# A transformer kernel's opening stage: weights loaded first, key slots parted into halves, and work moved between VectorE and ScalarE

## The chip, the cores and the metric

The kernel runs on one core of a Trainium2 chip. The metric is the device time of one execution in microseconds, as a median over runs. All arithmetic is fp32. Matrix products are made from split operands: each fp32 number is a rounded part (hi, in the fp32r format) and the rest (lo), and three products (hi x hi, lo x hi, hi x lo) stand for one.

## The reference, cut to what matters

The program is two transformer blocks over 256 tokens of width 2048, with 256 context tokens beside them in the first. The change touches the start of the first block:

```python
c_act = silu(c);  cc_act = silu(c_ctx)
mod = (c_act @ w_mod + b_mod)                 # 2048 -> 6 * 2048, for x
mod_c = (cc_act @ w_mod + b_mod)              # the same for the context
sh1, sc1, gt1, sh2, sc2, gt2 = split(mod, 6)
h  = rmsnorm(x,   g_norm1) * (1 + sc1)  + sh1
hc = rmsnorm(ctx, g_norm1) * (1 + csc1) + csh1
z  = h @ w_in                                 # keys, values, queries, gates of the mixers
```

rmsnorm divides by the root of the mean square over the 2048 features. So before the first key can be summed, the norm of x and ctx (the two streams, s = 0 and 1) and the first quarter of sh1 and sc1 must be there.

## The kernel before, in words

Weights come in slots of 1 MB (128 partitions x 2048 fp32). SyncE loads them into a ring of four raw buffers (RAW, `load`, L443 to L473). ScalarE rounds each half slot to hi (`front_split`, L537), VectorE subtracts to get lo (L1167), and TensorE uses both. There are two hi and two lo buffers of a slot each, so four halves can be ready or in use: the hi of half n waits until half n - 4 is used. A load waits until the second half of the slot that last held its raw buffer has been split (lo_ready). SyncE issues loads in one order, that of the first use of each slot, and waits in that order too.

The order of all halves is written out by hand in the list UNITS (L76 on). An entry is a kind, a number and a half, and its place in the list is called a unit here. Units 0 to 15 are the eight modulation slots of round 0; rounds 1, 2 and 3 have eight more each. A round gives one quarter of sh1 and sc1 for both streams. A modulation half is 4 matmuls of 128x512 on a 16-wide stationary operand (`mod_slot`, L2049, L2050), a key half 24 matmuls of 128x512 (`both`, L1965 to L1967). "key4" q is the part of four key columns that uses quarter q of the operand; "lr_key" 0 uses quarters 0 and 1. In the list of before each key4 slot stands whole: key4 0 at units 28 and 29, key4 1 and lr_key 0 at 46 to 49, key4 2 at 70 and 71, and then key 5 and key4 3.

All engines walk the same list. At each unit ScalarE and VectorE split the half four units further on (`ahead_of`), which on ScalarE waits until the present unit is used. Around that, at fixed places:

- Start: x and ctx are loaded in eight pieces of 0.5 MB ahead of all weights (L477). ScalarE squares them (L556), TensorE sums the squares over partitions with a matrix of ones (L2184), all ahead of the first modulation product. ScalarE takes the root at slot 1 (L515), VectorE the reciprocal at slot 3 (L1101).
- Norm product (L1319): two slots ahead of a round's end VectorE multiplies quarter r of both streams by the reciprocal root, 128x1024 each.
- End of a round: ScalarE copies the summed modulation rows out of PSUM (`mrows`, L572), TensorE turns them with eight small matmuls (`turn_rows`, L2057), VectorE adds the bias (`modulation`, L1179), makes the gain (`gains`, L1205) and applies the affine step, eight blocks of 128x256 (L1273, `operand_made`). ScalarE rounds the quarter of each stream to hi (L561, `operand_hi`), and VectorE makes the rest (L1280, `operand_rest`) one slot later, with two more lo halves between the two.

Of the kernel before, what the change touches and what calls it, by code (L numbers as in the profile page):

```python
# [23 lines left out]
ALU = mybir.AluOpType  # L24
ACT = mybir.ActivationFunctionType
AX = mybir.AxisListType.X

P = 128
# [47 lines left out]
UNITS = modulation_of(MODS[0] + MODS[1][:6]) + whole(("key4", 0)) + modulation_of(MODS[1][6:] + MODS[2][:6])  # L76
UNITS += whole(("key4", 1), ("lr_key", 0)) + modulation_of(MODS[2][6:] + MODS[3]) + whole(("key4", 2)) + [("key", 5, 0)]
# [25 lines left out]
LAST = [AT["mod", m[-1]] for m in MODS[:4]]  # L103
# [82 lines left out]
SHARED["made"] = [("x1", 8), ("y", 2), ("n2", 4), ("lat", 2)]  # L186
# [44 lines left out]
def build(nc, A, out):  # L231
    with ExitStack() as ctx:
        sems = {}

        def sem(name):
            if name not in sems:
                sems[name] = ctx.enter_context(nc.semaphore(name))
            return sems[name]
# [162 lines left out]
        def blk(t, j, n=1):  # L401
            return t[:, bass.ds(j * T, n * T)] if not isinstance(j, int) else t[:, j * T:(j + n) * T]
# [38 lines left out]
        def _(sp):  # L441
# [32 lines left out]

            for s in range(2):
                for q in range(4):
                    sp.dma_start(xs(xf, s, q), A["xt"][:, (s * KD + 4 * q) * T:(s * KD + 4 * q + 4) * T]).then_inc(sem(f"x_loaded{4 * s + q}"), 16)  # L477
            for t, (kind, k) in enumerate(FIRST_USE):
                load(t, t % RING, kind, k)
# [9 lines left out]
        def _(act):  # L489
# [63 lines left out]
            for s in range(2):  # L553
                for q in range(4):
                    act.wait_ge(sem(f"x_loaded{4 * s + q}"), 16)
                    act.activation(blk(sq[s], 4 * q, 4), xs(xf, s, q), ACT.Square).then_inc(sem("squares_ready"), 1)  # L556
            def operand_hi(r):

                for s in range(2):
                    act.wait_ge(sem("operand_made"), reached("made", "x1", 2 * r + s + 1))  # L560
                    act.activation(xs(xh, s, r), xs(xf, s, r), ACT.Copy).then_inc(sem("operand_hi"), 1)  # L561
# [3 lines left out]
            for u, (kind, k, half) in enumerate(UNITS):  # L565
                n = AT[kind, k]
                if half and n in LAST:
                    r = LAST.index(n)
# [4 lines left out]
                if (kind, k, half) == ("key4", 2, 1):  # L573
                    operand_hi(3)
# [7 lines left out]
                if n == 1:  # L582
                    root("n1", rsx[:, :], PS[4][:, :], D)
                for r in range(3):
                    if n == LAST[r] + 2:
                        operand_hi(r)

# [496 lines left out]
        def _(dve):  # L1084
# [179 lines left out]
            def operand_made(r):  # L1264

                modulation(r)
                for s in range(2):
                    gains(s, 16, s, "g1", 4 * r, 4)
                own.wait()
                for s in range(2):  # L1270
                    for b in range(4 * r, 4 * r + 4):
                        f = s * KD + b
                        ins = dve.tensor_scalar(blk(xf, f), blk(xf, f), amod[:, f:f + 1], mview[:, b, s:s + 1], ALU.mult, ALU.add)  # L1273
                    ins.then_inc(sem("operand_made"), 1)
# [20 lines left out]
            for u, (kind, k, half) in enumerate(UNITS):  # L1295
# [6 lines left out]
                if (kind, k, half) == ("key4", 2, 1):  # L1302
                    operand_made(3)
                    operand_rest(3)
                if UNITS[u] in HALF:
                    for m in ahead_of(u):
                        front_split(m)
                    if HALF[UNITS[u]] + 4 >= len(SPLITS) and not half:
                        split("mix_out", 0, (HALF[UNITS[u]] + 4 - len(SPLITS)) // 2, 0)
                if not half:  # L1310
                    continue
                if n == 3:
                    recip("n1", rsx[:, :])

                for r in range(4):
                    if n == LAST[r] - 2:
                        for s in range(2):
                            a = by_head(xs(xf, s, r))
                            own.done(dve.tensor_tensor(a, a, rsx[:, s * T:(s + 1) * T][:, None, :].to_broadcast([P, 4, T]), ALU.mult))  # L1319
                    if n == LAST[r] + 1 and r < 3:  # L1320
                        operand_made(r)
                    if n == LAST[r] + 2 and r < 3:
                        operand_rest(r)
# [224 lines left out]
            dve.wait_ge(sem("n2_gained"), 16)  # L1548
# [408 lines left out]
        def _(pe):  # L1957
# [222 lines left out]
            for s in range(2):  # L2180
                for b in range(KD):
                    if b % 4 == 0:
                        pe.wait_ge(sem("squares_ready"), reached("squares", "n1", 4 * s + b // 4 + 1))
                    ins = pe.matmul(PS[4][:, s * T:(s + 1) * T], ones[:, :], blk(sq[s], b), start=s + b == 0, stop=s == 1 and b == KD - 1,  # L2184
                                    skip_group_check=True)
            ins.then_inc(sem("norm_sum"), 1)
            pe.wait_ge(sem("c_ready"), 1)
            pe.wait_ge(sem("fold_ready"), 2)
            for t, (kind, k, half) in enumerate(UNITS):
# [43 lines left out]
                if AT[kind, k] - 1 in LAST and half == (kind != "key4"):  # L2233
                    turn_rows(LAST.index(AT[kind, k] - 1))
# [406 lines left out]
```

## Time and profile before

| | |
|---|---|
| Runs | 2837.6, 2826.0, 2834.99 us; median 2834.99 us |
| Profiled execution | 2836.49 us, span 2834.7 us, mean granted clock 0.979 |
| TensorE matmul busy | 2700.3 us (95%) |
| VectorE busy | 2027.8 us (72%) |
| ScalarE busy | 1421.4 us (50%) |
| DMA | 530.21 MB, mean 187 GB/s |

The stage that the change touches is the first 172 us. A busy share over the whole span says little of it; it is read by windows. "Idle before" a group is time in which its engine had nothing to do ahead of those instructions, with what ended it. The granted clock of TensorE is given as a share of its full 2.4 GHz; its other level is 0.5.

### The profile page before, as it was taken

How to read it: one execution, taken by the hardware profiler on the slowest of the kernel's cores; microseconds unless marked ns; L12 is line 12 of the kernel's file. 1: busy time of each engine (PE TensorE's matmuls, PEld its weight loads, DVE VectorE, ACT ScalarE, POOL GpSimd, SP SyncE). 2: the span in 40 equal slices, each digit the busy share in tenths (PEclk: the TensorE clock that was granted, in tenths of full speed). 3: DMA queues.
4: the chain of work that ended last, by engine and by line, in shares of the span. 5: the costliest groups of instructions: out<-in, count | busy, mean ns of one | idle time of the engine just before them, and what ended most of it. 6: DMA issues, size and time to landing. Idle time of an engine off the chain costs nothing.

```text
span 2834.7 us, 42305 instructions
## 1 busy us (share of the span) xinstructions
PE 2700.3 (95%) x15974; PEld 2343.9 (83%) x15974; DVE 2027.8 (72%) x3081; ACT 1421.4 (50%) x2000; POOL 0.2 (0%) x4
## 2 busy tenths in 40 slices
PE   7899999999979999999999999999999899999988
PEld 3468778998868888888888888889988898988877
DVE  6676786985878888887556777776654888456576
ACT  6433433444445555554444665554444654665563
POOL 0000000000000000000000000000000000000000
PEclk9999999999989999999999999999999999999989
DMA  8667565640735545455555455544555445432433
GB/s 345 226 250 268 228 258 220 220 186 31 268 137 189 191 179 191 181 191 175 189 189 189 170 186 191 179 172 182 183 188 183 146 160 186 165 136 109 178 139 129
DMA packets 104534, 530.21 MB, mean 187 GB/s; under 512 B 8240, under 2 KB 8784, under 8 KB 51296
## 3 DMA queue, kind: packets, MB, share of 16 engines
q1 hardware_dynamic: 101888, 515.93, 49.8%
q10 hardware_dynamic: 2528, 12.66, 1.2%
q8 instruction: 79, 1.29, 0.2%
q14 instruction: 39, 0.32, 0.0%
HBM read 526.46 MB, written 2.10 MB: 186 GB/s over the span
## 4 chain that ended last, share of the span: by engine, by line
PE 66%; DVE 7%; issue 3%; ACT 2%; ACTq 0%; DVEq 0%; DMA 0%
PE ps L1973 33%; PE ps L1974 16%; PE ps L1965 4%; PE ps L1967 4%; PE ps L1966 4%; DVE lo L1096 2%; ACT hi L503 1%; PE ps L2310 1%; DVE ws L1691 1%; PE ps L2481 1%; PE ps L2479 0%; PE ps L2315 0%; ACT L866 0%; DVE R L1739 0%; DVE O L1737 0%
## 5 line engine op out<-in xcount | busy, mean ns | idle before, releaser
L1096 DVE TENSOR_TENSOR lo<-raw,hi 128x1024 fp32r<-128x1024 f32 x700 | 843.3, 1222 | 480.5 <-ACT hi L503 477.7
L503 ACT ACTIVATE hi<-raw 128x1024 fp32r<-128x1024 f32 x700 | 732.3, 1056 | 615.6 <-PE ps L1974 547.1
L1973 PE MATMUL ps<-x,hi 128*128 128x512 f32 x1376 | 487.6, 400 | 0.0
L1974 PE MATMUL ps<-x,lo 128*128 128x256 f32 x1376 | 387.0, 281 | 0.0
L1973 PE MATMUL ps<-y,hi 128*128 128x512 f32 x1024 | 364.2, 400 | 3.6 <-DVE y L1943 3.6
L1973 PE MATMUL ps<-xp,hi 128*128 128x512 f32 x1024 | 358.6, 396 | 5.5 <-DVE lo L1096 3.7
L1973 PEld LDWEIGHTS ps<-x,hi 128*128 128x128 f32 x1376 | 259.3, 188 | 64.8
L537 ACT ACTIVATE hi<-raw 128x1024 fp32r<-128x1024 f32 x162 | 167.3, 1054 | 275.7 <-PE ps L1967 115.4
L1974 PE MATMUL ps<-y,lo 128*128 128x256 f32 x1024 | 288.9, 282 | 0.0
L1974 PE MATMUL ps<-xp,lo 128*128 128x256 f32 x1024 | 284.7, 278 | 0.0
L1167 DVE TENSOR_TENSOR lo<-raw,hi 128x1024 fp32r<-128x1024 f32 x162 | 192.5, 1220 | 104.8 <-ACT hi L537 104.7
L1974 PEld LDWEIGHTS ps<-x,lo 128*128 128x128 f32 x1376 | 260.6, 189 | 0.0
L1973 PE MATMUL ps<-hx,hi 128*128 128x512 f32 x688 | 243.1, 399 | 0.0
L1973 PEld LDWEIGHTS ps<-xp,hi 128*128 128x128 f32 x1024 | 192.0, 188 | 53.9 <-DVE lo L1096 6.9
L1973 PEld LDWEIGHTS ps<-y,hi 128*128 128x128 f32 x1024 | 194.0, 189 | 51.2 <-issue 4.1
L1974 PEld LDWEIGHTS ps<-y,lo 128*128 128x128 f32 x1024 | 195.3, 191 | 0.0
L1974 PE MATMUL ps<-hx,lo 128*128 128x256 f32 x688 | 193.2, 281 | 0.0
L1974 PEld LDWEIGHTS ps<-xp,lo 128*128 128x128 f32 x1024 | 192.6, 188 | 0.0
L1965 PE MATMUL ps<-xh,hi 128*128 128x256 f32 (+1 forms) x528 | 168.1, 318 | 5.6 <-ACT V L606 3.2
L1966 PE MATMUL ps<-xl,hi 128*128 128x256 f32 (+1 forms) x528 | 165.9, 314 | 0.0
L1967 PE MATMUL ps<-xh,lo 128*128 128x256 f32 (+1 forms) x528 | 165.8, 314 | 0.0
L1200 DVE SCALAR_TENSOR_TENSOR wsum<-raw,csil,wsum 128x512 f32<-128x512 f32 x210 | 157.6, 750 | 6.3
(385 smaller groups left out, 5015.3 us busy)
## 6 DMA issues: line engine op xcount, KB each, us to landing
raw<-in_weights SPq DMA_DIRECT2D x483, 1024.0 KB, 4.8
wlast<-in_weights ACTq DMA_DIRECT2D x8, 1024.0 KB, 4.8
xf<-in_xt SPq DMA_DIRECT2D x8, 512.0 KB, 9.5
raw<-in_weights SPq DMA_DIRECT2D x4, 768.0 KB, 4.3
R<-in_xt ACTq DMA_DIRECT2D x1, 2048.0 KB, 7.3
out<-R SPq DMA_DIRECT2D x1, 2048.0 KB, 6.3
maskn<-in_maskn ACTq DMA_DIRECT2D x1, 512.0 KB, 3.4
ptr<-in_pt ACTq DMA_DIRECT2D x2, 256.0 KB, 3.8
```

The lines of the kernel that those rows point to most:

```text
L503: act.activation(HI[p % PAIR][:, c], RAW[p % RING][:, c], ACT.Copy).then_inc(hi_ready, 1)
L537: act.activation(half_of(HI, n), RAW[t % RING][:, h * SLOT // 2:(h + 1) * SLOT // 2], ACT.Copy).then_inc(hi_ready, 1)
L1096: dve.tensor_tensor(LO[p % PAIR][:, c], RAW[p % RING][:, c], HI[p % PAIR][:, c].bitcast(F32), ALU.subtract).then_inc(lo_ready, 1)
L1167: dve.tensor_tensor(half_of(LO, n), RAW[t % RING][:, h * SLOT // 2:(h + 1) * SLOT // 2], half_of(HI, n).bitcast(F32), ALU.subtract).then_i ...
L1200: ins = dve.scalar_tensor_tensor(total[:, :], piece, scale, total[:, :], ALU.mult, ALU.add)
L1691: st.done(dve.tensor_tensor(dst[:, 16:UPW], src[:, 16:UPW], src[:, 16 - lag:UPW - lag], ALU.add))
L1965: pe.matmul(o, wh, ah, start=start, stop=False, **kw)
L1966: pe.matmul(o, wh, al, start=False, stop=False, **kw)
L1967: return pe.matmul(o, wl, ah, start=False, stop=stop, **kw)
L1973: pe.matmul(o, h, pair[:, :, k, :], start=start, stop=False, **kw)
L1974: return pe.matmul(o[:, 0, :], l, pair[:, 0, k, :], start=False, stop=stop, **kw)
L2310: pe.matmul(PS[4 + d][:, j * T:(j + 1) * T], W[:, t * T + j * P:t * T + (j + 1) * P], V[:, vc:vc + DV], start=(j, t) in ((0, 0), (1, 1 if ...
```

## The change

Five edits:

1. SyncE issues the first four weight slots ahead of the eight pieces of x. The squares and their sums, on ScalarE and TensorE, are parted into four groups of two pieces: squares after the splits made at units 1, 3, 5, 7, sums after units 3, 5, 7, 9. The root moves to unit 9 and the reciprocal to unit 11.
2. In UNITS the two halves of key4 0, key4 1, lr_key 0 and key4 2 are set apart, with modulation halves between. The second half follows the last modulation half of a round, at units 33, 45, 53 and 71 (45 is inside round 2). key4 0's first half is unit 26, key4 1's 40, lr_key 0's 48, key4 2's 64.
3. The rows of a round are turned inside the unit that follows the round, after two of its eight products where that is a key half, after the unit where it is a modulation half.
4. The affine step of stream 0 goes to ScalarE (four activations with scale and bias, 128x256 each, at the head of `operand_hi`); VectorE keeps stream 1. ScalarE waits for a new semaphore, gains_made. `operand_rest` follows `operand_made` directly, both at the unit behind the round.
5. The norm product of rounds 1 to 3 moves up to units 26, 40 and 48 (round 0: unit 13).

The core of the diff:

```diff
+UNITS = modulation_of(MODS[0] + MODS[1][:5]) + [("key4", 0, 0)] + modulation_of(MODS[1][5:]) + [("key4", 0, 1)]
+UNITS += modulation_of(MODS[2][:3]) + [("key4", 1, 0)] + modulation_of(MODS[2][3:5]) + [("key4", 1, 1)]
+UNITS += modulation_of(MODS[2][5:6]) + [("lr_key", 0, 0)] + modulation_of(MODS[2][6:]) + [("lr_key", 0, 1)]
+UNITS += modulation_of(MODS[3][:5]) + [("key4", 2, 0)] + modulation_of(MODS[3][5:]) + [("key4", 2, 1), ("key", 5, 0)]
...
+ENDS = [UNIT["mod", m[-1], 1] for m in MODS[:4]]
+NORMED_AT = [UNIT["mod", MODS[0][6], 1], UNIT["key4", 0, 0], UNIT["key4", 1, 0], UNIT["lr_key", 0, 0]]
+SQUARES_AT = [3, 5, 7, 9]
...
+            for t in range(RING):
+                load(t, t, *FIRST_USE[t])
             for s in range(2):
                 for q in range(4):
                     sp.dma_start(xs(xf, s, q), ...)
-            for t, (kind, k) in enumerate(FIRST_USE):
-                load(t, t % RING, kind, k)
+            for t in range(RING, len(FIRST_USE)):
+                load(t, t % RING, *FIRST_USE[t])
...
             def operand_hi(r):
+                act.wait_ge(sem("gains_made"), r + 1)
+                for b in range(4 * r, 4 * r + 4):
+                    ins = act.activation(blk(xf, b), blk(xf, b), ACT.Identity, scale=amod[:, b:b + 1], bias=mods[:, 2 * b:2 * b + 1])
+                ins.then_inc(sem("n2_gained"), 1)
...
+                if u - 1 in ENDS:
+                    operand_hi(ENDS.index(u - 1))
+                if u in ENDS:
+                    r = ENDS.index(u)
                     act.wait_ge(halves_used, HALF[kind, k, half] + 1)
                     if r:
                         act.wait_ge(sem("mod_turned"), r)
                     act.activation(mrows[:, :], PS[6 + r % 2][0:16, :], ACT.Copy).then_inc(sem("mod_rows"), 1)
                 if UNITS[u] in HALF:
                     for m in ahead_of(u):
                         front_split(m)
+                if u + 2 in SQUARES_AT:
+                    x_squares(SQUARES_AT.index(u + 2))
+                if u == SQUARES_AT[-1]:
+                    root("n1", rsx[:, :], PS[4][:, :], D)
...
             def operand_made(r):
                 modulation(r)
-                for s in range(2):
-                    gains(s, 16, s, "g1", 4 * r, 4)
+                gains(1, 16, 1, "g1", 4 * r, 4)
+                dve.scalar_tensor_tensor(amod[:, 4 * r:4 * r + 4], mview[:, 16 + 4 * r:20 + 4 * r, 0], 1.0, v("g1", 4 * r, 4),
+                                         ALU.add, ALU.mult).then_inc(sem("gains_made"), 1)
...
                 pe.wait_ge(lo_ready, m + 1)
                 for n in range(count // 2):
+                    if n == 2 and u - 1 in ENDS:
+                        turn_rows(ENDS.index(u - 1))
...
+                if t - 1 in ENDS and kind == "mod":
+                    turn_rows(ENDS.index(t - 1))
+                if t in SQUARES_AT:
+                    x_sums(SQUARES_AT.index(t))
```

`x_squares(n)` squares pieces 2n and 2n + 1 of x; `x_sums(n)` is eight of the 32 matmuls with ones.

## Rows read from the trace of the kernel before

**Rows 1.** The page: the span.
```profile
span 2834.7 us, 42305 instructions
```

**Rows 2.** Windows by round: stretch and length, busy time by engine, PEclk, DMA share, GB/s.
```profile
22.87:46.28 23.41, 18.21 (x66) 5.73 (x64) 21.51 (x18) 17.37 (x18) 0.00 (x0) 0.93 0.91 363
46.28:82.16 35.88, 29.91 (x121) 16.01 (x120) 27.29 (x34) 20.67 (x22) 0.00 (x0) 0.90 0.71 263
82.16:129.86 47.70, 40.12 (x169) 24.89 (x168) 30.76 (x37) 22.66 (x24) 0.00 (x0) 0.96 0.61 220
129.86:155.93 26.07, 18.50 (x72) 6.78 (x72) 25.72 (x33) 17.77 (x19) 0.00 (x0) 0.93 0.79 293
155.93:171.80 15.87, 13.47 (x56) 10.99 (x57) 10.77 (x19) 5.51 (x6) 0.00 (x0) 0.89 0.48 173
171.80:300.00 128.20, 128.20 (x660) 108.07 (x658) 93.62 (x116) 45.10 (x54) 0.00 (x0) 1.00 0.69 267
```

**Rows 3.** Groups of TensorE, 0 to 200 us: busy, mean ns | idle before.
```profile
L2049 PE MATMUL ps<-hi,cwin 128*16 128x512 f32 x128 | 55.0, 430 | 26.3 <-DVE lo L1167 25.9
...
L2057 PE MATMUL ps<-fold,mrows 16*128 16x8 f32 x32 | 4.2, 254 | 0.0
```

**Rows 4.** Timeline of ScalarE, 18 to 38 us: start, length, instruction, idle before.
```profile
18.99 2.00 ACT L537 ACTIVATE hi<-raw 128x1024 fp32r<-128x1024 f32 x2 [1.43 <-DMA raw<-in_weights]
...
28.47 1.28 ACT L515 ACT_TABLE_LOAD   x1
29.76 0.69 ACT L515 ACTIVATE rsx<-ps,vec 128x512 f32<-128x512 f32 x1
...
36.99 2.00 ACT L537 ACTIVATE hi<-raw 128x1024 fp32r<-128x1024 f32 x2 [0.46 <-DMA raw<-in_weights]
```

**Rows 5.** Groups of VectorE by form, 0 to 200 us.
```profile
L1167 DVE TENSOR_TENSOR lo<-raw,hi 128x1024 fp32r<-128x1024 f32 x80 | 93.4, 1219 | 50.0 <-ACT hi L537 49.8
...
L1273 DVE TENSOR_SCALAR xf<-xf,amod,mods 128x256 f32<-128x256 f32 x32 | 10.7, 406 | 0.1
...
L1101 DVE RECIPROCAL rsx<-rsx 128x512 f32<-128x512 f32 x1 | 3.3, 3343 | 0.0
...
L1205 DVE SCALAR_TENSOR_TENSOR amod<-mods,vec 128x4 f32<-128x4 f32 x8 | 0.9, 159 | 0.1
```

**Rows 6.** Groups of ScalarE by form, 0 to 200 us; L787 from the whole span.
```profile
L572 ACT ACTIVATE mrows<-ps 16x512 f32<-16x512 f32 x4 | 2.3, 570 | 0.0
...
L787 ACT ACTIVATE x<-tn,mods 128x256 fp32r<-128x256 f32 x16 | 6.7, 496 | 5.4 <-DVE tn L1552 5.4
```

**Rows 7.** Windows of TensorE: norm sums, four key halves, four modulation halves.
```profile
11.30:22.80 11.50, 11.50 (x55) 1.00 1.02 420
104.48:126.16 21.68, 21.68 (x97) 1.00 0.51 187
126.24:129.86 3.62, 3.62 (x16) 1.00 0.27 36
```

**Rows 8.** Loads of L473, issue to landing: 117 to 129 us, then 22 to 37 us.
```profile
DMA to landing us min/median/max: 4.7/4.7/4.7
...
DMA to landing us min/median/max: 5.6/6.4/7.0
```

**Rows 9.** Timeline of VectorE, 36 to 200 us: where the halves of each round stand.
```profile
43.91 2.35 DVE L1319 TENSOR_TENSOR xf<-xf,rsx 128x1024 f32<-128x1024 f32 x2
...
60.66 5.76 DVE L1167 TENSOR_TENSOR lo<-raw,hi 128x1024 fp32r<-128x1024 f32 x5
...
97.54 6.89 DVE L1167 TENSOR_TENSOR lo<-raw,hi 128x1024 fp32r<-128x1024 f32 x6
...
145.24 6.89 DVE L1167 TENSOR_TENSOR lo<-raw,hi 128x1024 fp32r<-128x1024 f32 x6
```

**Rows 10.** TensorE at unit 70: first matmul in the timeline, window over the half.
```profile
158.33 0.77 PE L1965 MATMUL ps<-xh,hi 128*128 128x512 f32 x1 [2.40 <-DVE lo L1167]
...
158.33:165.42 7.09, 7.09 (x25) 0.79 0.74 258
```

More of the change, by code:

```diff
@@ L102 @@
 UNIT = {e: n for n, e in enumerate(UNITS)}
-LAST = [AT["mod", m[-1]] for m in MODS[:4]]
+ENDS = [UNIT["mod", m[-1], 1] for m in MODS[:4]]
+NORMED_AT = [UNIT["mod", MODS[0][6], 1], UNIT["key4", 0, 0], UNIT["key4", 1, 0], UNIT["lr_key", 0, 0]]
+SQUARES_AT = [3, 5, 7, 9]
 NEXT_GATE = {n - 1: k for n, (kind, k) in enumerate(FRONT) if kind == "gate"}
@@ L185 @@
 SHARED["whole"] = [("up", KF), ("pool_in", 64), ("mla_in", 14), ("ple1", 16)]
-SHARED["made"] = [("x1", 8), ("y", 2), ("n2", 4), ("lat", 2)]
+SHARED["made"] = [("x1", 4), ("y", 2), ("n2", 4), ("lat", 2)]
 for _k in ("hi", "x"):
@@ L552, in _, with x_squares @@
             act.activation(csil[:, :], v("c2", 0, 2 * KD), ACT.Silu).then_inc(sem("c_act"), 1)
-            for s in range(2):
-                for q in range(4):
-                    act.wait_ge(sem(f"x_loaded{4 * s + q}"), 16)
+            def x_squares(n):
+                for m in (2 * n, 2 * n + 1):
+                    s, q = m // 4, m % 4
+                    act.wait_ge(sem(f"x_loaded{m}"), 16)
                     act.activation(blk(sq[s], 4 * q, 4), xs(xf, s, q), ACT.Square).then_inc(sem("squares_ready"), 1)
             def operand_hi(r):
+                act.wait_ge(sem("gains_made"), r + 1)
+                for b in range(4 * r, 4 * r + 4):
+                    ins = act.activation(blk(xf, b), blk(xf, b), ACT.Identity, scale=amod[:, b:b + 1], bias=mods[:, 2 * b:2 * b + 1])
+                ins.then_inc(sem("n2_gained"), 1)
                 for s in range(2):
-                    act.wait_ge(sem("operand_made"), reached("made", "x1", 2 * r + s + 1))
+                    if s:
+                        act.wait_ge(sem("operand_made"), reached("made", "x1", r + 1))
+                    else:
+                        act.wait_ge(sem("n2_gained"), r + 1)
                     act.activation(xs(xh, s, r), xs(xf, s, r), ACT.Copy).then_inc(sem("operand_hi"), 1)
@@ L566, in _ @@
                 n = AT[kind, k]
-                if half and n in LAST:
-                    r = LAST.index(n)
+                if u - 1 in ENDS:
+                    operand_hi(ENDS.index(u - 1))
+                if u in ENDS:
+                    r = ENDS.index(u)
                     act.wait_ge(halves_used, HALF[kind, k, half] + 1)
@@ L572, in _ @@
                     act.activation(mrows[:, :], PS[6 + r % 2][0:16, :], ACT.Copy).then_inc(sem("mod_rows"), 1)
-                if (kind, k, half) == ("key4", 2, 1):
-                    operand_hi(3)
                 if UNITS[u] in HALF:
@@ L579, in _ @@
                         split("mix_out", 0, (HALF[UNITS[u]] + 4 - len(SPLITS)) // 2, 0)
+                if u + 2 in SQUARES_AT:
+                    x_squares(SQUARES_AT.index(u + 2))
+                if u == SQUARES_AT[-1]:
+                    root("n1", rsx[:, :], PS[4][:, :], D)
                 if not half:
                     continue
[L582 to L586, printed above, removed]
                 if (kind, k) == ("key4", 3):
@@ L1266, in operand_made @@
                 modulation(r)
-                for s in range(2):
-                    gains(s, 16, s, "g1", 4 * r, 4)
+                gains(1, 16, 1, "g1", 4 * r, 4)
+                dve.scalar_tensor_tensor(amod[:, 4 * r:4 * r + 4], mview[:, 16 + 4 * r:20 + 4 * r, 0], 1.0, v("g1", 4 * r, 4),
+                                         ALU.add, ALU.mult).then_inc(sem("gains_made"), 1)
                 own.wait()
[L1270 to L1274, printed above, removed]
+                for b in range(4 * r, 4 * r + 4):
+                    f = KD + b
+                    ins = dve.tensor_scalar(blk(xf, f), blk(xf, f), amod[:, f:f + 1], mview[:, b, 1:2], ALU.mult, ALU.add)
+                ins.then_inc(sem("operand_made"), 1)
             def operand_rest(r):
@@ L1301, in _ @@
                     level_arg(m)
-                if (kind, k, half) == ("key4", 2, 1):
-                    operand_made(3)
-                    operand_rest(3)
+                if u - 1 in ENDS:
+                    operand_made(ENDS.index(u - 1))
+                    operand_rest(ENDS.index(u - 1))
                 if UNITS[u] in HALF:
@@ L1309, in _ @@
                         split("mix_out", 0, (HALF[UNITS[u]] + 4 - len(SPLITS)) // 2, 0)
+                if u == SQUARES_AT[-1] + 2:
+                    recip("n1", rsx[:, :])
+                if u in NORMED_AT:
+                    r = NORMED_AT.index(u)
+                    for s in range(2):
+                        a = by_head(xs(xf, s, r))
+                        ins = dve.tensor_tensor(a, a, rsx[:, s * T:(s + 1) * T][:, None, :].to_broadcast([P, 4, T]), ALU.mult)
+                        own.done(ins)
                 if not half:
                     continue
[L1312 to L1323, printed above, removed]
                 for g, end in enumerate(GROUP_ENDS):
@@ L1547, in _ @@
             recip("n2", rs[:, :])
-            dve.wait_ge(sem("n2_gained"), 16)
+            dve.wait_ge(sem("n2_gained"), 20)
             for q in range(5):
@@ L2179, in _, with x_sums @@
             pe.wait_ge(sem("ones_ready"), 1)
[L2180 to L2186, printed above, removed]
+            def x_sums(n):
+                for m in (2 * n, 2 * n + 1):
+                    pe.wait_ge(sem("squares_ready"), reached("squares", "n1", m + 1))
+                    s, q = m // 4, m % 4
+                    for b in range(4 * q, 4 * q + 4):
+                        ins = pe.matmul(PS[4][:, s * T:(s + 1) * T], ones[:, :], blk(sq[s], b), start=s + b == 0, stop=s == 1 and b == KD - 1,
+                                        skip_group_check=True)
+                if n == 3:
+                    ins.then_inc(sem("norm_sum"), 1)
             pe.wait_ge(sem("c_ready"), 1)
@@ L2231, in _ @@
                     half_slot(t, lambda n, h, l: one_stream(k % 2, n, h, l))
-                if AT[kind, k] - 1 in LAST and half == (kind != "key4"):
-                    turn_rows(LAST.index(AT[kind, k] - 1))
+                if t - 1 in ENDS and kind == "mod":
+                    turn_rows(ENDS.index(t - 1))
+                if t in SQUARES_AT:
+                    x_sums(SQUARES_AT.index(t))
                 if not half:
```

2 lines of the change are left out of this document (removed).

## The prediction

> **What bounds the kernel now.** I read the page first [rows 1], for the span against which the sum is made: 2834.7 us, in an execution that took 2836.49 us, 1.5 us above the median shown (2834.99). Then the windows [rows 2], cut where one modulation round ends and the next begins, since the diff touches nothing behind unit 71. From 171.8 us on TensorE has no free time (128.20 us busy of 128.20): what is won or lost ahead of that point passes whole into the span. Ahead of it TensorE is not the bound. Between 22.87 and 46.28 us VectorE is busy 21.51 of 23.41 us, between 129.86 and 155.93 us it is 25.72 of 26.07 us. In the two middle rounds it idles only while a key slot is on TensorE. The groups of TensorE [rows 3] say the same from the other side: 26.3 us idle ahead of modulation products, 25.9 us of that until a lo half was ready. Those 26 us are all that the change can win: 0.9% of the span. The start has a third bound, the DMA engines: the first weight slot lands at 18.99 us, the eighth at 36.99 us [rows 4], so (36.99 - 18.99) / 7 = 2.57 us for each MB.
>
> **Prices.** A lo half is 1.22 us alone [rows 5], 6.89 / 6 = 1.15 us in a row; the norm product is 2.35 us for both streams [rows 9]; one affine block is 10.7 / 32 = 0.33 us, a small operation on gains 0.16 us, the reciprocal 3.34 us [rows 5]. On ScalarE a hi half is 2.00 / 2 = 1.0 us [rows 4], the modulation rows 0.57 us, and a scaled, biased block of the same shape, from a later stage, 6.7 / 16 = 0.42 us [rows 6]. On TensorE a half of a key slot is 21.68 / 4 = 5.4 us, a modulation half 3.62 / 4 = 0.91 us, and the norm sums, at full clock, 11.50 / 55 = 0.21 us a record, so 3.4 us for the 16 records of one of the four new groups [rows 7]. Turning the rows is 4.2 / 4 = 1.05 us [rows 3]. A load that finds the queue empty lands 4.7 us after its issue [rows 8]; behind others 2.5 us more each.
>
> **Weights ahead of x, and norm sums between units 3 and 9.** The bytes ahead of slot 4 are the same 8 MB in either order. With 2.57 us for each MB and the first MB at about 7 us (an estimate from the same rate, counted back), slots 0 to 3 land by 17 us, x by 27 us, slot 4 at about 29 us and slot 7 at about 37 us, as now. That is why the early start wins nothing by itself. But ScalarE rounds both halves of slot 4 (to 31.4 us) ahead of x's third pair of squares (to 33.4), slot 5's halves (to 35.4) ahead of the fourth (to 37.4). TensorE sums the third pair to 35.9 us, does units 8 and 9 (to 37.8) and sums the fourth to 41.2. The root (0.7 us) stands on ScalarE ahead of the halves of slot 7, so these are split at 45.2 us and the reciprocal ends at 48.6 us. Before, VectorE had as many halves and the reciprocal behind it at 43.91 us [rows 9]. **Loss: 4.7 us** of VectorE time. The table load goes ahead of root's wait (1.28 us [rows 4]), so I put it at nothing. What the page would add: the Trainium skill, ScalarE: Activation LUTs, section What ACT_TABLE_LOAD costs, counts a drain of some 1.4 us with each switch; the rows show none, root starting as the load ends, and with it this term would be 6.1 us.
>
> **Half of the affine step on ScalarE.** VectorE loses four blocks a round (4 x 0.33 = 1.3 us). But operand_rest now follows operand_made at once, with no lo halves between them, and its first half waits for ScalarE: four blocks (1.7 us), a hi (1.0 us) and two hand-overs (0.2 us) behind gains_made, against 1.3 us of VectorE's own blocks. VectorE idles about 1.6 us, so the term is +0.3 us a round. Behind this wait stand all further splits of VectorE, and ScalarE, waiting for gains_made, holds back its own. Bounds: -1.3 us a round (the wait hidden) and +1.6 us (nothing saved).
> First anchor: the rests of round 0 end at 48.6 + 4 halves 4.6 + norm product 2.3 + four small operations 0.6 + 1.3 + wait 1.6 + two rests 2.3 = 61.3 us with 20 halves split; before, 60.66 us with 24 [rows 9]. Lag 0.6 + 4 x 1.15 = 5.2 us.
>
> **Key quarters in two halves.** The intention is plain: while TensorE works 5.4 us on a key half, VectorE catches up. With four buffers for halves it can be three ahead (3.4 us) and then idles, once per half instead of once per slot. So each half hides 3.4 us, and a slot parted hides twice that. Against it stand three things. The norm product for the next quarter comes behind the split that waits for this very key half (unit 30 behind 26), so its 2.3 us lie beside short modulation halves, not under the key. Second, raw slot 13 of the order, the first key quarter, is now held from unit 26 to 33; SyncE waits in order, so the load for units 34 and 35 is issued only when unit 33 is split. Third, that lands ahead of a wait: ScalarE's list has the rounding of units 34 and 35 ahead of the copy of the modulation rows of unit 32, and TensorE now asks for those rows inside unit 33, two products in. Counting from unit 29 used: hi 1.0 + lo 1.2 + load 4.7 + two hi 2.0 + rows 0.6 + hand-overs 0.3 (an estimate from the gaps of some 0.1 us in these rows) = 9.8 us, while TensorE has three modulation halves (2.8 us) and a quarter of a key half (1.4 us). It stands still for 5.6 us or more there.
> - Round 1 walked so: units 20 to 29 split at 73.2, unit 30 at 77.2, norm product 79.5, units 31 to 33 at 82.9; load lands 87.7, rows copied 90.4 (TensorE has waited since 84.3), rests end at 98.0 us with 37 halves. Before: 97.54 us with 42 [rows 9]. Lag 0.5 + 5 x 1.15 = 6.2 us. The stall costs little because VectorE was behind as well.
> - Round 2: unit 53 releases the load for unit 56, which is behind the rows, so TensorE is not held, but VectorE is (3.7 us). Two key slots are parted here and give that back. Rests end at 145.3 us with 57 halves; before 145.24 us with 62 [rows 9]. Lag 5.8 us.
> - Round 3: unit 71 is split at 165.7 us; it releases the load for units 72 and 75, and the one for 73 and 74 stands behind it. Both are rounded ahead of the rows of unit 70: 4.7 + 2.5 + 1.0 + 0.6 + 0.3 puts the rows at 174.8 us, while TensorE has stood in unit 71 since 167.2. Turning 1.05 and the other 18 of 24 products 4.1 end unit 71 at 180.0 us. Before: 171.8 us. **Lag: 8.2 us**, and from here on TensorE has no slack to take it up.
>
> **The clock.** The 171.8 us of before hold one slow stretch: the key half from 158.33 us took 7.09 us at a granted clock of 0.79, 1.7 us over the price at full clock, behind 2.40 us of idle time [rows 10]. With 7.6 us of standing still in unit 71 I expect at least such a stretch behind it: +1.6 us. In the other rounds TensorE is not the bound, and slow halves cost nothing.
> By the Trainium skill, TensorE: Matmul & The Clock Gate, section HAM oscillation, waits between short bursts of products bring the engine back to its half clock again and again. By that rule each stall of the new order pays; the row agrees in kind, and with two such stretches instead of one the sum would be 1.6 us more.
>
> **Sum:** 4.7 (start) + 0.5 + 1.0 - 0.4 + 2.4 (rounds 0 to 3) = 8.2 us, + 1.6 us for the clock = 9.8 us on 2836.49 us, or about 2845 us against the median. A difference within 0.5% (14 us) is about what a measurement of this kernel cannot tell from none.
> **Bounds.** Low: the halves of slots 4 and 5 come early and the start loses nothing (-4.7), the clock stays up (-1.6), ScalarE's blocks are hidden (-1.3 a round in two rounds): +1. High: the two loads that hold the rows take 6.4 us as those behind others do [rows 8] (+3.4), a second slow stretch (+1.6), the affine term at its upper bound (+2.6): +17.
>
> **Rivals.**
> - *It works* (12%): the split key halves hide VectorE, and the rows are copied in time. For it: the 25.9 us of idle time are there, and VectorE is idle 35.88 - 27.29 = 8.6 us in round 1, which has one key slot [rows 2]. Against it: the order of ScalarE's list. Half of the idle time back gives 2822 us, nearly all 2811.
> - *The stalls add in full* (17%): the decisive place is the copy of the modulation rows behind the held loads. If VectorE is not behind at the two held rows, TensorE's waits of 6 and 7.6 us stand for themselves on top of the start's 4.7 us: with the clock 4.7 + 5.6 + 7.6 + 1.6 = 20 us, 2855 us. It decides once the load is not landed when unit 32 or 70 is used.
> - *No effect* (18%): the start's loss is not there, since the squares come ahead of slot 4 by chance of landing, or later TensorE time takes it up; +3 us, 2838 us. For it: VectorE's total work hardly changes (-5.2 us of blocks, + waits). Against: x's squares stand behind slot 4 in ScalarE's list.
> - My forecast, 53%: 2845 us, by itself 2837 to 2853.
>
> **Numbers.** The range 2831 to 2856 takes in the no-effect case and the edge of the full stalls. Slower by over 14 us holds a fifth of the forecast and most of the second rival: 0.22. Faster by over 14 us needs over half of the idle time back: 0.07. The rest, 0.71, lies within.
>
> **What would show it.** Right: slot 7 landing at 37 us as before; root and reciprocal later by some 10 us; one idle stretch of TensorE of about 6 us inside unit 33 and one of 7 us inside unit 71, each ended by the copy of the rows, with a raw load as ScalarE's own releaser; VectorE idle 1 to 2 us ahead of the first rest of each round; the unbroken TensorE work starting near 180 us. Wrong: the copy of rows within 1 us of the last product of its round, or unbroken work starting ahead of 172 us.

## The result, and the profile after

The changed kernel took 2854.22 us in the median of seven runs (2843.0 to 2861.1), the one before 2834.99 us (2818.0 to 2837.6). The ratio is 1.0076, with a 95% interval of 1.0049 to 1.0104: 0.8% slower, some 21 us (14 to 30). On a second chip it was 1.0102 (1.0069 to 1.0134). The forecast was 2845 us, slower by 10 us. The direction was right, the size was half of what came.

Behind the changed stage every kernel of this study, the one before too, falls on one of two levels some 10 us apart, so single times say little here and the stage itself was measured in the traces (last section).

The page's span, after:

```profile
span 2857.3 us, 42305 instructions
```

The windows of the changed kernel, cut at the last modulation half of rounds 1, 2 and 3 and at the end of unit 71. Columns as in [rows 2].

```profile
46.28:84.09 37.81, 27.57 (x96) 12.83 (x96) 31.37 (x33) 19.43 (x23) 0.00 (x0) 0.82 0.42 165
84.09:136.72 52.63, 43.07 (x168) 27.79 (x168) 30.02 (x33) 26.12 (x29) 0.00 (x0) 0.87 0.58 220
136.72:173.01 36.29, 32.10 (x121) 17.40 (x120) 27.10 (x30) 21.04 (x24) 0.00 (x0) 0.91 0.61 232
173.01:189.60 16.59, 9.11 (x33) 7.40 (x33) 7.08 (x13) 7.62 (x10) 0.00 (x0) 0.69 0.65 253
189.60:300.00 110.40, 110.40 (x585) 94.54 (x584) 76.87 (x94) 37.45 (x45) 0.00 (x0) 1.00 0.69 269
```

No window is full on any engine until 189.60 us, where before it was so from 171.80 us [rows 2]. In round 1 the share of the DMA engines' time fell from 0.71 to 0.42 although ScalarE waits for loads (below): they are issued late. The stage ends 17.7 us later, as the first TensorE product that reads wsum shows (wsum holds later modulation weights times silu(c), summed on VectorE, and TensorE reads it first behind the stage). It stands in unbroken TensorE work in both kernels, at 233.13 us here and at 215.43 us before, and it is the measure of all experiments. In timeline rows of the changed kernel:

```profile
233.13 0.94 PE L2079 MATMUL ps<-ones,wsum 128*128 128x1 f32 x8
```

The waits of ScalarE name the cause. For 80 to 190 us in the changed kernel, then for 80 to 172 us in the one before (who waited for what: us, times, longest):

```profile
ACT hi L543 <- DMA raw<-in_weights: 40.7, 12, 10.3
ACT hi L543 <- PE ps L1977: 9.0, 5, 3.4
```

```profile
ACT hi L537 <- PE ps L1967: 22.7, 5, 5.2
ACT hi L537 <- PE ps L2050: 12.4, 10, 2.1
ACT xh L561 <- DVE xf L1273: 6.1, 6, 3.1
ACT hi L537 <- DMA raw<-in_weights: 2.5, 2, 1.4
```

Before, ScalarE waited mostly until a buffer was used (22.7 + 12.4 us) and 2.5 us for loads; now it waits 40.7 us for loads. The groups of TensorE (busy, mean ns | idle before) tell where the loads held it; the first is answered by [rows 3]:

```profile
L2061 PE MATMUL ps<-hi,cwin 128*16 128x512 f32 x128 | 55.6, 434 | 23.4 <-DVE lo L1181 23.1
...
L2069 PE MATMUL ps<-fold,mrows 16*128 16x8 f32 x32 | 7.5, 358 | 14.4 <-ACT mrows L590 14.4
```

The idle time ahead of modulation products hardly shrank (26.3 to 23.4 us), and 14.4 us of a new wait came: for the copy of the modulation rows. The timeline of ScalarE around unit 33 shows the order that was feared: two roundings that wait for a load, then the rows.

```profile
76.07 3.90 ACT L543 ACTIVATE hi<-raw 128x1024 fp32r<-128x1024 f32 x4 [4.15 <-PE ps L1977]
90.31 2.00 ACT L543 ACTIVATE hi<-raw 128x1024 fp32r<-128x1024 f32 x2 [10.33 <-DMA raw<-in_weights]
92.22 0.57 ACT L590 ACTIVATE mrows<-ps 16x512 f32<-16x512 f32 x1
```

And TensorE, inside units 33 and 71:

```profile
92.84 1.87 PE L2069 MATMUL ps<-fold,mrows 16*128 16x8 f32 x8 [7.01 <-ACT mrows L590]
...
182.12 1.87 PE L2069 MATMUL ps<-fold,mrows 16*128 16x8 f32 x8 [7.35 <-ACT mrows L590]
```

Each turning takes 1.87 us here, against 4.2 / 4 = 1.05 us before: the granted clock was 0.50 by then.

### The profile page after: what moved, and what is told of

Read it like the earlier page. It is cut to its first block, busy times and chain, and to the rows that moved or that the text cites. A ratio compares the mean times of both kernels' runs of the same rounds, so it can differ in the third digit from the quotient of the medians.

```text
span 2857.3 us, 42305 instructions
## 1 busy us (share of the span) xinstructions
PE 2713.3 (95%) x15974; PEld 2355.5 (82%) x15974; DVE 2024.3 (71%) x3065; ACT 1428.7 (50%) x2016; POOL 0.2 (0%) x4
## 4 chain that ended last, share of the span: by engine, by line
PE 66%; DVE 7%; issue 3%; ACT 3%; ACTq 0%; DVEq 0%
PE ps L1983 32%; PE ps L1984 17%; PE ps L1975 4%; PE ps L1976 4%; PE ps L1977 4%; DVE lo L1110 2%; ACT hi L509 1%; PE ps L2329 1%; DVE ws L1701 1%; PE ps L2500 1%; PE ps L2498 0%; PE ps L2334 0%; ACT L880 0%; ACT L509 0%; DVE R L1749 0%
```

## The experiments

Where the first wsum product stood, in all profiles:

| Kernel | us |
|---|---|
| before, two profiles | 215.4, 213.7 |
| after, two profiles | 233.1, 234.7 |
| after, start as before (a1) | 229.5 |
| after, key slots whole (a2) | 221.8 |
| after, affine step on VectorE (a3) | 232.7 |
| after, rows first (a4) | 232.0 |
| after, whole operand step first (a5) | 223.6 |
| after, half loads, two profiles (a6, c2) | 214.4, 217.5 |
| half loads, start as before, two profiles (a8, c3) | 209.0, 211.9 |
| the same, affine step on VectorE (a9) | 209.0 |
| half loads, old start, norm products ahead (b1) | 203.2 |
| changed order, old start, affine step on VectorE (d1) | 227.2 |
| new start, key slots whole, affine step on VectorE (d2) | 223.6 |

All but the pairs are one profile each, and two profiles of one kernel lie 1.6 to 3.2 us apart; differences under some 3 us are not told apart here.

**a1: the start undone.** The loads of x go ahead of all weights again, and the squares and sums of x stand where they stood.

```diff
-            for t in range(RING):
-                load(t, t, *FIRST_USE[t])
             for s in range(2):
...
+            for n in range(4):
+                x_squares(n)
-                if u == SQUARES_AT[-1]:
+                if u == 3:
                     root("n1", rsx[:, :], PS[4][:, :], D)
-                if u == SQUARES_AT[-1] + 2:
+                if u == 7:
                     recip("n1", rsx[:, :])
```

> The changed kernel, with only the start as before: x ahead of all weights, its squares and norm sums ahead of the first modulation product, root at unit 3, reciprocal at unit 7. Measure: the first TensorE product that reads wsum, at 215.4 us before and 233.1 us after (lag 17.7 us). My theory (the start costs VectorE 4.7 us, which nothing takes up later): about 228.5 us. Rival (TensorE's two waits inside units 33 and 71 set the end of the stage, and a later VectorE only fills them): 233 us, the stage as late as after. Third (the start of the change is a gain that the rest gives back): later than 234 us.

229.47 us: 3.7 us less than the first profile of the changed kernel, 5.3 us less than the second. The start is a loss of that size and nothing later takes it up. TensorE still stands 7.05 and 7.33 us ahead of the turnings of rounds 1 and 3.

**a2: key slots whole.**

```diff
-UNITS = modulation_of(MODS[0] + MODS[1][:5]) + [("key4", 0, 0)] + ...
+UNITS = modulation_of(MODS[0] + MODS[1][:6]) + whole(("key4", 0)) + ...
-NORMED_AT = [UNIT["mod", MODS[0][6], 1], UNIT["key4", 0, 0], UNIT["key4", 1, 0], UNIT["lr_key", 0, 0]]
+NORMED_AT = [UNIT["mod", MODS[0][6], 1], 29, 49, 65]
```

> The changed kernel, with only the order of units as before (each key slot whole), and the norm products of rounds 1 to 3 at units 29, 49 and 65. Start, affine half on ScalarE and place of the turning as changed. My theory (parted slots hold their raw buffer, the loads behind them come late and in bursts of four): first wsum product at 215.4 + 4.7 (start) + about 1 to 2 (the wait of VectorE for ScalarE) = 221 to 222 us, and no idle stretch of TensorE over 4 us behind the first modulation round. Rival (the wait for ScalarE in the affine step and the start carry the lag): 229 us or more.

221.81 us, as expected. One idle stretch of TensorE over 4 us is left behind the first round (4.79 us ahead of 64.03 us), where I had expected none; the changed kernel has it too. The order of units, with the places of the norm products, is worth 11 to 13 us of the lag.

**a3: the affine step back on VectorE.** `operand_made` does both streams, `operand_hi` only rounds; the rests follow at once.

> The changed kernel, with only the affine step of stream 0 back on VectorE. VectorE does eight blocks a round again, ScalarE rounds the quarters behind them, the rests follow at once. My theory (the term is a wash, +0.3 us a round by my sum): first wsum product within 1.5 us of 233.1 us. Rival (the wait for ScalarE costs 1.9 us in each round and all of it counts): 226 to 229 us. Rival (the blocks taken off VectorE are a real gain): 236 to 238 us.

232.71 us. The wash holds. In the changed kernel's timeline of VectorE it can be read: 1.38 us of blocks instead of 2.67, and 1.89 us of waiting for ScalarE behind them.

```profile
55.53 1.38 DVE L1287 TENSOR_SCALAR xf<-xf,amod,mods 128x256 f32<-128x256 f32 x4
58.80 2.36 DVE L1294 TENSOR_TENSOR xl<-xf,xh 128x1024 fp32r<-128x1024 f32 x2 [1.89 <-ACT xh L577]
```

**a4: the rows ahead of the held roundings, on ScalarE alone.**

```diff
                     act.activation(mrows[:, :], PS[6 + r % 2][0:16, :], ACT.Copy).then_inc(sem("mod_rows"), 1)
+                    if r % 2:
+                        front_split(u + 2)
+                        front_split(u + 3)
...
                     for m in ahead_of(u):
-                        front_split(m)
+                        if m - 2 not in ENDS[1::2] and m - 3 not in ENDS[1::2]:
+                            front_split(m)
```

> The changed kernel, with only ScalarE's order changed at the ends of rounds 1 and 3: the modulation rows are copied ahead of the roundings of units 34, 35 and 72, 73, which wait for late loads. My theory: TensorE's waits of 7.0 and 7.35 us inside units 33 and 71 go, the half clock behind them too; but VectorE still makes the operand behind the late halves, so in round 1 little is won (1 to 2 us), and in round 3 the wait moves to unit 73, 5 us shorter. First wsum product at 226 to 228 us. Rival (the waits are all of the lag behind the start): 219 us. Rival (VectorE and the loads set everything): 232 us or later.

231.99 us. My 226 to 228 us was wrong. The rows were copied in time (85.62 us), both waits at the turning went, and 1 us came of it, which is inside the scatter. TensorE stood elsewhere instead: 6.05 us for a lo half at 103.03 us, 4.55 us at 153.95 us, 4.03 us for the operand's rest at 192.12 us. VectorE's timeline shows why: its own queue had the same lo halves ahead of the operand step.

```profile
92.11 3.72 DVE L1185 TENSOR_TENSOR lo<-raw,hi 128x1024 fp32r<-128x1024 f32 x3 [7.26 <-ACT hi L543]
95.75 0.23 DVE L1197 TENSOR_TENSOR mods<-ps,vec 128x8 f32<-128x8 f32 x2
```

So the stall that is easiest to see, TensorE inside units 33 and 71, was not what cost the time.

**a5: the whole operand step ahead of the held splits, on both engines.** As a4, and now `operand_hi(r)` on ScalarE, `operand_made(r)` and `operand_rest(r)` on VectorE stand ahead of the same splits in rounds 1 and 3.

> The changed kernel, with the whole operand step of rounds 1 and 3 (rows copied, affine step, hi, rests) ahead of the splits of units 34, 35 and 72, 73 on ScalarE and on VectorE alike, so that both engines use the time in which the held loads land. Measure: first TensorE product that reads wsum, 233.1 us after the change, 232.0 us with the rows alone moved. Theory now (behind the held loads stand not the rows alone but VectorE's operand step too): 5 us won in round 1 and 4 in round 3, so 223 to 226 us. Rival (the late loads themselves set the pace, whatever stands behind them): 230 us or more, since units 34 and 35 are as late as before.

223.60 us, 8.4 us less than with the rows alone. The dependent work had been queued behind late loads on two engines; it has to pass them on both. The loads are late still, and the stage still ends some 9 us behind before's.

**a6: half loads.** Each parted slot becomes two loads of 0.5 MB, each into a raw buffer of its own. The bytes are the same.

```diff
+PARTED = [("key4", 0), ("key4", 1), ("lr_key", 0), ("key4", 2)]
+LOADS = [(kind, k, half if (kind, k) in PARTED else None) for kind, k, half in UNITS if not half or (kind, k) in PARTED]
...
+                    if part is not None:
+                        words = words[:, 2 * part:2 * part + 2, :]
+                        stored = A["weights"][w + 2 * part:w + 2 * part + 2, :, 512 * k:512 * (k + 1)].rearrange("a p c -> p a c")
...
-                t = FIRST_USE.index((kind, k))
+                t = LOADED[UNITS[u]]
```

> The changed kernel, with each of the four parted slots loaded as two loads of half a slot, each into a raw buffer of its own at its own place of the load order. The bytes are the same; no raw buffer is held over other units any more, and no load waits for a parted slot. Order of units, start, affine half and turning as changed. Theory (the held raw buffers make the lag behind the start): the waits of 7.0 and 7.35 us inside units 33 and 71 are gone, and the first wsum product is at 217 to 221 us (215.4 + 4 of the start, + 0 to 1). Rival (the order of units itself, with its norm products beside short halves, costs the time): 228 us or more.

214.35 us: 18.8 us earlier, and earlier than I had dared (217.53 us in the second profile, still 15.6 us ahead of the changed kernel's better one). The order of units, the turning, the start and the affine half are those of the change. No raw buffer is held over other slots any more. A parted load is also half as long, which the run does not tell apart; at the 2.5 us for each MB seen here that is some 1.3 us a load, 10 us if each of the eight counted in full (an estimate), less than the 18.8 us. The waits of ScalarE from 80 to 172 us and the turnings on TensorE:

```profile
ACT hi L555 <- PE ps L1989: 16.4, 5, 6.8
ACT xf L582 <- DVE amod L1294: 9.2, 3, 5.3
ACT hi L555 <- DMA raw<-in_weights: 8.5, 5, 2.9
```

```profile
L2081 PE MATMUL ps<-fold,mrows 16*128 16x8 f32 x32 | 5.3, 288 | 2.4 <-ACT mrows L602 2.4
```

8.5 us of waits for loads stand where 40.7 us stood, 2.4 us ahead of the turnings where 14.4 us stood.

**a8 and a9: half loads with the old start; then the affine step on VectorE as well.**

> As the one with half loads, and the start as before as well. Theory (start and held buffers are the whole lag, and each adds): first wsum product at 213 to 217 us, that is within 2 us of the kernel before. If parting the keys is a gain of its own where nothing is held: 205 to 211 us. Rival (the two do not add): 219 us or more.

> As the last one, and the affine step of stream 0 back on VectorE. With the held loads gone the wait of VectorE for ScalarE (1.9 us in each round) is no longer covered by another. Theory (the term is a wash whatever stands beside it): within 1.5 us of the last one. Rival (the wait counts where VectorE is the bound): 2 to 5 us earlier than it. Rival (the freed blocks count there): 2 to 5 us later.

209.02 and 209.00 us. My 213 to 217 us for a8 was too late; its second case, 205 to 211 us, came. Start and held buffers add, and the affine step is a wash without cover as well. Once nothing is held, the new order of work is a gain: 6.4 us between the first profiles, 4.1 us between the means of two (210.5 against 214.6 us).

**b1: the norm products ahead of their unit's split.** In a8 TensorE still stood 2.2 to 2.3 us behind each of three key halves.

```diff
+                if u in NORMED_AT[1:]:
+                    normed_quarter(NORMED_AT.index(u))
                 if u - 1 in ENDS:
                     operand_made(ENDS.index(u - 1))
...
-                if u in NORMED_AT:
+                if u in NORMED_AT[:1]:
```

> The kernel with half loads and the old start, and the norm products of rounds 1 to 3 moved ahead of the split of their unit on VectorE, so that they run while TensorE is in the key half instead of behind it. Theory (three idle stretches of TensorE of 2.2 to 2.3 us behind key halves are these products): they go, and the first wsum product is 4 to 6 us earlier than 209.0 us, at 203 to 205 us; against the kernel before 0.3 to 0.6% faster. Rival (the stretches are the handing on of one half by ScalarE and VectorE): no change, 209 us.

203.19 us. Its time is 0.9961 (0.9934 to 0.9987) of that of the kernel before: some 11 us faster (4 to 19), by a stage that ends 10.5 to 12.2 us earlier. In the timeline of VectorE the product now starts as the splits in hand are done, and ahead of the half that waits for the key:

```profile
68.86 2.35 DVE L1292 TENSOR_TENSOR xf<-xf,rsx 128x1024 f32<-128x1024 f32 x2
72.29 6.90 DVE L1191 TENSOR_TENSOR lo<-raw,hi 128x1024 fp32r<-128x1024 f32 x6 [1.08 <-ACT hi L553]
```

**c1, c2, c3: timed, on the chip of b1.**

> The changed kernel once more, on the chip of the others. First wsum product within 1 us of 233.1 us. Behind it the time falls on two levels some 10 us apart, as in the runs so far (2607.8 to 2615.8 us in five, 2619.3 to 2624.2 us in four), whatever the kernel; if that is so, the ratio to before is 1.006 to 1.009 with both levels in both kernels. If the lag of 4.8 us behind unit 71 were part of the change, its runs would be on the upper level alone.

1.0102 (1.0069 to 1.0134), above my range. Its stage ends at 234.72 us, 1.6 us behind the first profile and not within 1 us of it, and behind it the profile is on the lower level (2610.6 us), so the 4.9 us that the first profile lost behind the stage (2624.2 against 2619.3 us) are not of the change. 0.0102 is 29 us (20 to 38), more than the stage's lag; by their times four of the changed kernel's six runs were on the upper level and ten of before's 29, which may be the rest. With so few runs that is not shown.

> The changed kernel with half loads, timed. First wsum product at 214.4 us, 1 us ahead of before: ratio to before 0.997 to 1.001. If its one look (2824.4 us against 2835.0) told the truth and not the level of that run, 0.996.

1.0003 (0.9981 to 1.0026), with the stage at 217.53 us, 3.2 us later than in the first profile. On the same chip the changed kernel had 1.0102: the half loads take the loss away in the times too.

> Half loads and the old start, timed. First wsum product at 209.0 us, 6.4 us ahead of before: ratio 0.996 to 0.999.

1.0003 (0.9977 to 1.0029), above my 0.996 to 0.999. The gain of some 4 us that its stage shows (209.0 and 211.9 us) is inside the interval; the gain that I had expected is not shown by the times.

**d1 to d3: the parts put in one at a time, and the kernel before once more.**

> Of the change only the parted order, the place of the turning and the earlier norm products: start as before, affine step of both streams on VectorE (rests directly behind it). If the parts add: first wsum product at 215.4 + 17.7 - 4 (start) - 0.4 (affine) = 228 to 229.5 us, with two idle stretches of TensorE of 6 to 7.5 us inside units 33 and 71. If the holding is only costly behind a late start: 222 us or less.

> Of the change only the new start (four slots ahead of x, squares, sums, root and reciprocal between the units), with key slots whole and both streams' affine step on VectorE. By my step of the prediction: 215.4 + 4.7 = 220.1 us, up to 221.7 us if the clock is halved once more at the start, as in the profiles with a stretch near 32 us. Rival (without the parted order the late reciprocal is taken up by a key slot): 216 us.

> The kernel before, profiled once more. First wsum product within 1 us of 215.4 us, and behind it 2607 to 2616 us or 2619 to 2624 us, one of the two levels. If it comes at 212 to 213 us, the missing 2 to 4 us lie in the stage, since its first profile was a slow one.

d1 227.24 us, with waits of 5.7 and 7.4 us at the turnings; d2 223.60 us, behind my 220.1 to 221.7; d3 213.73 us, neither within 1 us of 215.4 nor at 212 to 213.

The cleanest pair is d1 and a9: the two kernels differ by the half loads alone, and a9's stage ends 18.2 us earlier (209.00 against 227.24 us).

Against the mean of the two profiles of before (214.6 us) d1 is 12.7 us later and d2 9.0 us, more than the 4 to 5 us that a1 gave for the start. Together that is 21.7 us, against 19.3 us for the change whole (233.9 us in the mean). Neither kernel has its part quite alone. Both, d2 too, also hold edit 3 and the rests directly behind the affine step at the unit behind a round, which before does not. So the place of the operand step is counted in both, while a1, measured against the changed kernel, leaves it out. d2's 9.0 us may be the start and that place together, or a start that costs more where key slots are whole; no run has the place alone, and it stays open. A half-speed stretch of the clock of 6.8 us from 165 us on in d2 is one small part (before has one of 3.4 us at the same unit).

The lag of the stage is 17.7 to 21.0 us from one pair of profiles to another, and the 21 us of the first ratio agree with it. The end of the stage moves by 1.7 us between the profiles of before and by 1.6 to 3.2 us between those of others. The later profiles of c1, c2 and c3 have one or two stretches of half clock more than the first ones, but d3 has one more than before's first and ended earlier, so the clock does not account for it.

## Why the prediction was right and wrong

The walk of the prediction can be laid beside the trace:

| Step | foretold | traced |
|---|---|---|
| reciprocal ends | 48.6 | 48.2 |
| rests of round 0 end | 61.3 | 61.2 |
| TensorE stands in unit 33 | 84.3 to 90.4 | 85.8 to 92.8 |
| rests of round 1 end, 37 halves | 98.0 | 101.1 |
| rests of round 2 end, 57 halves | 145.3 | 151.9 |
| TensorE stands in unit 71 | 167.2 to 174.8 | 174.8 to 182.1 |
| unit 71 ends, with the clock | 181.6 | 189.6 |

Turned into lags behind the kernel before as the prediction did it (a half missing counts 1.15 us; before 60.66 us with 24 halves, 97.54 with 42, 145.24 with 62, unit 71 at 171.8), the table gives what each term was worth:

| Term | foretold | traced |
|---|---|---|
| start and round 0 | 4.7 + 0.5 = 5.2 | 5.1 |
| round 1 | +1.0 | +4.2 |
| round 2 | -0.4 | +3.1 |
| round 3, with the clock | +2.4 + 1.6 = 4.0 | +5.4 |
| together | 9.8 | 17.8 |

**Right.** That the early start wins nothing: slot 4 landed at 28.43 us (29 foretold) and slot 7 at 35.88 us (37), while VectorE had 16 halves and the reciprocal behind it 4.3 us later than before (4.7). That the affine step is a wash (a3, a9). That the copy of the rows would stand behind held loads in rounds 1 and 3 and nowhere else, with 6 and 7.6 us of waiting (7.0 and 7.35). That TensorE's unbroken work starts later and keeps the lag.

**Wrong: the term of the key quarters.** Rounds 0 to 3 stood at 0.5 + 1.0 - 0.4 + 2.4 = 3.5 us, with the clock 5.1 us. With the start undone (a1) 229.5 - 214.6 = 14.9 us are left, and d1 is 12.7 us behind before. The steps that failed are the +1.0 us of round 1 and the -0.4 us of round 2 ("Two key slots are parted here and give that back"): the traces show +4.2 and +3.1 us. Round 3 was sized 1.4 us too low. The sentence "The stall costs little because VectorE was behind as well" holds for TensorE's own stall, as a4 shows; but VectorE waited for the same held loads, 7.33 us in one piece in round 1, 4.85 and 2.48 us in round 2, and that was priced too low. These things were mis-sized.
- A held buffer blocks more than one load. The four behind unit 33 were all issued within 1.3 us. SyncE's group in the changed kernel from 84 to 85.5 us, issue to landing, where [rows 8] gave 4.7 us for a load alone:

```profile
L477 SPq DMA_DIRECT2D raw<-in_weights x4: 328/431/647, 84.1 to 85.4; - x4
...
DMA to landing us min/median/max: 6.2/9.3/12.5
```

  The first took 6.2 us, not 4.7, the others came 2.5 us apart. Of the 3.1 us by which the walk missed round 1, 1.5 us are this, and 1.2 us were there already when unit 33 was split (84.06 us, 82.9 foretold). From 118.3 us the same happened in round 2 (6.0 us for the first, 3.7 us more for the second), at unit 45, a release for which the walk has no wait at all. In round 3 the first took 4.8 us, as priced.
- The high bound of the prediction had the 6.4 us, but only for the two loads ahead of the rows. The lag that the late loads make is VectorE's: the walk missed 3.1 us in round 1 and 3.5 us more in round 2.
- The clock. The prediction says that the 171.8 us of before hold one slow stretch. That was a misreading: the granted clock is under 1.00 in all five windows of [rows 2] ahead of 171.80 us, and 1 us windows show five stretches at 0.50, from about 41, 58, 99, 147 and 157 us on. The changed kernel has six, some 44 us together against 20. The stage of before, then of the changed kernel, from 22.87 us to its end:

```profile
22.87:171.80 148.93, 120.21 (x482) 64.40 (x481) 116.04 (x137) 84.00 (x86) 0.00 (x0) 0.93 0.70 261
22.87:189.60 166.73, 132.62 (x508) 78.33 (x507) 106.34 (x116) 90.92 (x102) 0.00 (x0) 0.87 0.60 233
```

  Two of the six are 10.24 us long and began while TensorE stood inside units 33 and 71:

```profile
88.14:98.38 10.24, 5.54 (x17) 4.75 (x18) 5.31 (x11) 6.33 (x9) 0.00 (x0) 0.50 1.00 402
176.88:187.12 10.24, 5.00 (x16) 4.30 (x17) 5.40 (x11) 5.90 (x9) 0.00 (x0) 0.50 0.79 318
```

  In unit 33 the 18 products behind the turning took 6.1 us instead of 4.1, in unit 71 5.7, and each turning 0.8 us more: 2.4 us in round 3, where TensorE sets the end, against the 1.6 us foretold. What the stretches cost in the other rounds was not measured; a4 has 37.5 us of half clock, a5 27.3 us and d2 40.9 us, and a5 and d2 end at the same time, so the lag does not follow them. By the Trainium skill (TensorE: Matmul & The Clock Gate, section HAM oscillation), which the prediction weighed, waits between short bursts of products bring the engine back to its half clock again and again. Both traces agree, with five stretches at 0.50 before and six after.

The rival "The stalls add in full" had the size (20 us) and not the reason: its 20 us are luck, since a4 took the stalls out and won 1 to 2 us. Its point of decision, the copy of the rows, is one symptom; the held raw buffers are the cause (18.8 us from the changed kernel to a6, 18.2 us from d1 to a9), and they delay VectorE through late hi halves as much as TensorE through late rows (a5). "No effect" fails by a1 and d2, "It works" by both profiles of the changed kernel, though a8 and b1 show that the idea was sound once the ring is not blocked: some 4 us of the stage, which the times do not show, and with the norm products ahead 11 us, which they do.

## What to carry to other kernels

Before the two halves of a slot are set apart in an order of work, ask what holds its buffer in between and what an in-order queue has behind that buffer: here one held raw buffer of four stopped all later loads, and its release sent four at once. Loading each part by itself, same bytes, turned a stage that ended 13 us late (d1) into one that ended 4 to 6 us early (a9, a8). And when a visible stall is taken away and the time stays, look at the next engine's queue for the same late operand before the theory is given up.

## What the runs showed of the hardware

In these runs TensorE has two speeds at a granted clock of 1.00. In the stretch from 1100 to 1300 us all kernels run the same instructions, without a gap. The windows of before, after, a6 and c1, in this order:

```profile
1100.00:1300.00 200.00, 200.00 (x1134) 173.38 (x1133) 171.80 (x302) 104.29 (x162) 0.00 (x0) 1.00 0.51 184
```

```profile
1100.00:1300.00 200.00, 200.00 (x1134) 173.50 (x1133) 171.04 (x300) 105.02 (x161) 0.00 (x0) 1.00 0.52 187
```

```profile
1100.00:1300.00 200.00, 200.00 (x1156) 176.34 (x1155) 175.03 (x309) 106.12 (x163) 0.00 (x0) 1.00 0.53 189
```

```profile
1100.00:1300.00 200.00, 200.00 (x1155) 176.36 (x1154) 174.93 (x308) 106.45 (x163) 0.00 (x0) 1.00 0.53 189
```

1134 or 1135 products in 200 us, or 1155 to 1157, 1.9% apart, and nothing between in the seventeen profiles. The changed kernel was at one speed here in its first profile and at the other in c1, the kernel before likewise (d3 had 1156), so it is not of the kernel. Nor is it of the whole execution. From 1650 to 1800 us, again without a gap, before's first profile is the faster one and d3 the slower:

```profile
1650.00:1800.00 150.00, 150.00 (x867) 131.18 (x866) 106.80 (x175) 88.76 (x121) 0.00 (x0) 1.00 0.51 187
```

```profile
1650.00:1800.00 150.00, 150.00 (x851) 130.03 (x850) 108.40 (x178) 86.47 (x117) 0.00 (x0) 1.00 0.52 182
```

The part behind the stage takes 2605.6 to 2615.8 us in the eleven profiles with the faster products from 1100 to 1300 us, and 2619.3 to 2624.2 us in the six with the slower ones. In before's first profile and in d3 the rate holds from 900 to 1500 us; 1.9% of those 600 us is 11 us, which is most of the step between the levels (an estimate from these counts). What chooses the speed was not found. For a change worth 10 us it means that the stage has to be read in the trace.
